# A two-layer hybrid decoder step: index products in units 3 and 4, digits in units 6 to 11, value rows placed on halves of x's parts

## The reference, cut to what matters

```
q, k, v, qi, ki, wi = split(x @ w_in)          # 14 tiles of 128 columns, and 328 more
s = einsum('bqhe,bse->bqhs', qi, ki)           # 8 index heads of width 64
score = einsum('bqhs,bqh->bqs', relu(s), wi) * IDX_SCALE
score = where(key <= query, score, NEG)
_, idx = top_k(score, topk)                    # prompt: 128 of up to 512, sample: 256 of 1025
logits = q . k[idx] * ATTN_SCALE + t5_bias(table, q_pos - idx)
out = softmax(logits) . v[idx]                 # GQA: 16 heads, 4 key heads
x = LN(ALPHA * x + out @ w_out); x = LN(ALPHA * x + relu(x @ w1)^2 @ w2)
```

## Time and profile before

| | |
|---|---|
| median of 3 runs | 1260.26 us |
| the profiled execution's own time | 1260.9 us |
| its span | 1259.1 us |
| PE busy | 1205.1 us (96%), 9582 matmuls |
| DVE busy | 709.0 us (56%) |
| ACT busy | 475.1 us (38%) |
| POOL busy | 82.2 us (7%) |
| mean granted TensorE clock | 0.985 |

### The profile page before, as it was taken

The page is one execution under the profiler, slowest core; times in us unless marked ns, Lnnn a source line. Parts: engine busy times, 40 slices in busy tenths (PEclk is TensorE's granted clock), DMA queues, the critical chain, the costliest instruction groups (busy, mean ns, idle before and its releaser), DMA issues.

```text
span 1259.1 us, 25585 instructions
## 1 busy us (share of the span) xinstructions
PE 1205.1 (96%) x9582; PEld 1109.9 (88%) x9582; DVE 709.0 (56%) x1456; ACT 475.1 (38%) x872; POOL 82.2 (7%) x118
## 2 busy tenths in 40 slices
PE   8998979999999999999999999799999999999995
PEld 4958845589899999999999987598999999999994
DVE  2288889857843443342457767678633433433477
ACT  2342137744532331331334476634422322322332
POOL 4334300100021000000000000000000000000000
PEclk9999989999999999999999999899999999999998
DMA  6687482043222222222233211131222222222221
GB/s 203 192 272 257 124 265 52 21 140 111 68 82 85 96 88 88 96 85 99 84 97 109 82 54 51 52 118 51 68 94 90 87 98 85 99 83 100 84 85 68
DMA packets 61958, 131.00 MB, mean 104 GB/s; under 512 B 7819, under 2 KB 34603, under 8 KB 61755
## 3 DMA queue, kind: packets, MB, share of 16 engines
q1 hardware_dynamic: 47899, 115.16, 28.0%
q10 hardware_dynamic: 10624, 8.26, 2.2%
q0 software_dynamic: 3360, 6.56, 1.7%
HBM read 125.41 MB, written 9.79 MB: 107 GB/s over the span
## 4 chain that ended last, share of the span: by engine, by line
PE 72%; DVE 12%; issue 6%; POOLq 3%; ACT 2%; POOL 2%; SPq 1%; DMA 1%; DVEq 0%; ACTq 0%
PE PS L604 56%; PE PS L634 7%; PE PS L1019 2%; PE PS L792 2%; PE PS L779 2%; PE PS L806 2%; DVE YA L1641 2%; SPq L394 1%; DVE YA L1628 1%; POOLq L385 1%; DVE RSTD L1633 1%; POOL IK L407 1%; POOLq L405 1%; DMA KVX<-cacheV 1%; DVE X L1647 1%
## 5 line engine op out<-in xcount | busy, mean ns | idle before, releaser
L1484 DVE TENSOR_TENSOR WLO<-WRAW,WHI 128x1024 fp32r<-128x1024 f32 x118 | 145.3, 1232 | 322.1 <-ACT WHI L1083 322.0
L1083 ACT ACTIVATE WHI<-WRAW 128x1024 fp32r<-128x1024 f32 x126 | 133.4, 1059 | 390.7 <-PE PS L604 356.9
L604 PE MATMUL PS<-XH,WHI 128*128 128x260 f32 x1184 | 242.3, 286 | 0.9 <-DVE XL L1809 0.7
L604 PE MATMUL PS<-XH,WLO 128*128 128x260 f32 x1184 | 239.9, 285 | 0.0
L604 PE MATMUL PS<-XL,WHI 128*128 128x260 f32 x1184 | 239.8, 284 | 0.0
L604 PE MATMUL PS<-HH,WHI 128*128 128x260 f32 x944 | 191.5, 284 | 0.2 <-DVE HL L1508 0.2
L604 PE MATMUL PS<-HH,WLO 128*128 128x260 f32 x944 | 190.4, 283 | 0.0
L604 PE MATMUL PS<-HL,WHI 128*128 128x260 f32 x944 | 190.2, 283 | 0.0
L604 PEld LDWEIGHTS PS<-XH,WHI 128*128 128x128 f32 x1184 | 183.5, 190 | 6.4 <-issue 5.4
L604 PEld LDWEIGHTS PS<-XH,WLO 128*128 128x128 f32 x1184 | 184.1, 190 | 0.0
L604 PEld LDWEIGHTS PS<-XL,WHI 128*128 128x128 f32 x1184 | 183.6, 190 | 0.0
(11 more groups left out here) (293 smaller groups left out, 1860.5 us busy)
## 6 DMA issues: line engine op xcount, KB each, us to landing
WRAW<-wall SPq DMA_DIRECT2D x168, 512.0 KB, 3.3
bias_skewed<-bias_seq SPq DMA_DIRECT2D x4, 1280.0 KB, 18.7
X<-xT SPq DMA_DIRECT2D x4, 520.0 KB, 6.6
X<-xT SPq DMA_DIRECT2D x1, 2080.0 KB, 11.4
yT<-X SPq DMA_DIRECT2D x8, 260.0 KB
KVB<-cacheK SPq DMA_DIRECT2D x16, 128.0 KB, 3.1
KVX<-cacheK SPq DMA_DIRECT2D x16, 128.0 KB, 2.9
KVB<-cacheK POOLq DMA_DIRECT2D x16, 128.0 KB, 7.3
```

Source lines behind the costliest of these rows:

```text
L604: mm = pe.matmul(PS[:, 2 * slot + g, 0:TG], w[:, slot, k, :], x[:, k, TG * g:TG * g + TG], start=(k == 0 and w is WHI and x is hi), stop=( ...
L1083: nc.scalar.activation(WHI[:, slot], WRAW[:, slot], ACT.Copy).then_inc(hi_done, 1)
L1484: V.tensor_tensor(WLO[:, slot], WRAW[:, slot], WHI[:, slot].bitcast(F32), ALU.subtract).then_inc(lo_dve, 1)
```

## The change

- The index items go head first (the three tiles of head 0, then of head 1, ...): 12 in unit 3 and 12 in unit 4, three at a time at every other piece of a unit, instead of 24 in unit 5. The transposed keys are evicted one unit earlier on ACT.
- The samples' scores and their sum over heads stand within unit 5, ahead of its pieces 2 and 4, instead of ahead of and within unit 6.
- The digits take slots 1 to 11 without a gap (units 6 to 11) instead of 2 to 9 and 12 to 14 (units 7 to 13). ACT reads its page numbers behind the samples' scores instead of ahead of them.
- DVE's low parts of units 4 to 7 stand elsewhere among its work, and the top-k rounds are dealt out anew: 9 rounds before the digits (before: 10), half a round at each digit and step (a whole one, two at the first step), 22 between MSK and QB (5), 5 behind QB (7), 3 (8) and half a round in each attention step from step 5 on (from step 2 on).
- Two of the value samples (8 and 10, `V_HALF`) lie wholly in the first half of XH and of XL; their pages are loaded once the first half of unit 13 has been multiplied. The bias of the diagonal blocks of t = 1 is copied by ACT from BT0 instead of being loaded with the rest, and the load of the rest comes behind the eviction of the samples' probabilities, of which the small one (PNEW) now comes first and has a semaphore of its own.

```diff
-V_LATE = (8, 9, 10, 11, 13, 14, 15)
+V_HALF, V_LATE = (8, 10), (9, 11, 13, 14, 15)
-SLOT_OF = (2, 3, 4, 5, 6, 7, 8, 9, 12, 13, 14)
+SLOT_OF = (1, 2, 3, 4, 5, 6, 7, 8, 9, 10, 11)
...
+        def load_first_values(eng, q, numbers):
+
+            eng.wait_ge(x_used, 1)
+            for n in V_HALF:
+                load_sample(eng, q, n, numbers)
...
+                    if u == A_OUT - 1 and k == KT // 2 - 1:
+                        mm.then_inc(x_used, 1)
...
-            items = [(t, h) for t in range(1, QT) for h in range(IDXH)]
+            items = [(t, h) for h in range(IDXH) for t in range(1, QT)]
...
-                if u == 5:
-                    between = {k: (lambda k=k: index_scores(3 * k, 3 * k + 3))
-                               for k in range(KT)}
-                elif u == 6:
-                    between = {2: sample_sums}
+                if u in (3, 4):
+                    n = 12 * (u - 3)
+                    between = {k: (lambda n=n + 3 * k // 2: index_scores(n, n + 3))
+                               for k in range(0, KT, 2)}
+                elif u == 5:
+                    between = {2: sample_scores, 4: sample_sums}
...
-            act.wait_ge(toe_skew, 16 * 4)
-            act.wait_ge(kv_used, DB)
-            load_bias(1)
             act.wait_ge(dt_mm, 1)
+            nc.scalar.activation(PNEW[:], PS[0:DB, 6, 0:P], ACT.Copy).then_inc(dt_ev, 1)
             nc.scalar.activation(PTD[:].rearrange("p k r -> p (k r)"), PSF[:, 2048:2048 + 1024],
-                                 ACT.Copy)
-            nc.scalar.activation(PNEW[:], PS[0:DB, 6, 0:P], ACT.Copy).then_inc(dt_ev, 1)
+                                 ACT.Copy).then_inc(dt_ev, 1)
+            act.wait_ge(toe_skew, 16 * 4)
+            load_bias(1)
...
-            for u in range(2, 6):
+            for u in range(2, 4):
                 low_part(u, u % 2)
...
-                if n == 8:
-                    low_part(6, 0)
-                if n == 16:
-                    sample_queries()
+                if n == 4:
+                    low_part(4, 0)
+                if n == 13:
+                    low_part(5, 1)
...
-            prompt_rounds(10)
-            low_part(7, 1)
+            low_part(6, 0)
+            prompt_rounds(9)
             dve.wait_ge(ds_ev, 1)
             for r in range(DIGITS):
...
-                prompt_rounds(1)
+                prompt_halves(1)
+                if r == 0:
+                    low_part(7, 1)
                 dve.wait_ge(r_dig, r + 1)
...
-                prompt_rounds(1 if i else 2)
+                prompt_halves(1)
...
-            prompt_rounds(5)
+            prompt_rounds(22)
             dve.wait_ge(z_qb, 2)
...
-            prompt_rounds(7)
+            prompt_rounds(5)
...
                 if i == -1:
-                    prompt_rounds(8)
-                elif i >= 2:
+                    prompt_rounds(3)
+                elif i >= 5:
                     prompt_halves(1)
```

More of the change, by code:

```diff
@@ L213, in program @@
         XL = place("XL", [P, KT, TOK], F32R)
-        KVR = place("KVR", [P, 4, NPG, 256], at=xw)
+        KVR = [place(f"KVR{n}", [P, NPG, 256], at=xw + n * KT // 2 * TOK) for n in range(4)]
         BT = place("BT", [P, NH, 512], at=xw + 16640)
@@ L506, in _ @@
             load_sample(sp, 0, 12, numbers)
+            load_first_values(sp, 0, numbers)
             load_values(sp, 0, numbers)
```

50 lines of the change are left out of this document (32 added, 18 removed).

## The result

| | before | after |
|---|---|---|
| median | 1261.55 us (4 runs, 1258.29 to 1264.9) | 1276.15 us (4 runs, 1272.9 to 1276.68) |
| profiled execution: own time, span | 1260.9, 1259.1 us | 1275.96, 1274.0 us |
| granted clock, mean | 0.985 | 0.982 |

The changed kernel is slower: ratio 1.0109, 95% interval 1.0089 to 1.0128. I had forecast 1264.2 us with a range to 1270, with 0.48 on slower, so the sign of the likeliest case was right, the size 12 us short.

The account below looks back on a forecast made before the run. PE, busy 96% of the span, was taken as the bound. Terms 15.2 + 1.8 - 2.25 - 3.1 - 2.1 - 3.7 - 2.6 = +3.3 us on the profiled 1260.9 gave 1264.2 us, range 1257 to 1270.

Parts of the forecast that it names:

- The change moves them and adds none: Units 3 and 4: the 24 index items cost PE 13.7 us, as they did in unit 5, with no wait added.
- unit 9's delay: Unit 9's load issued at 109.3, weights landing 4.2 us later, start at 117.3: 1.6 us lost.
- the late landings: Rival case: units 9 and 10 take 8.5 us to land, each gap costs 1.7 us of half clock; 1269 us, chance 0.17.
- the pace of the slots: Units 8 to 11: PE's slots set the digits, 3.1 us per half unit with its digit; eleventh at 137, MSK ready at 138.2.
- The 1.88 of before: PE's wait for the indicator at 127.54 goes, against about 1.8 us of new waiting between eighth digit and first step.
- The wait for QB: Ahead of the key products: 22 rounds put QB at 167.5, PE idles 13.7 us, key products start 15.2 us later.
- The half clock at the key products: The beginning of the key products runs at half clock behind the idling: +1.8 us (0 to 3.6).
- PD, first value products and values: Behind the key products: PD's wait goes (-2.25 us), first value products fall to 3.65 (-2.1), the wait on values goes (-3.7).
- POOL's low part of unit 8: Stays at 105.43 for 2.35 us, so unit 8 starts at 107.8 as before, with longer idling in front.
- either about 1.7 us or nothing: Cost in lost clock of one PE idle gap, read from the gaps ahead of unit 8 and of the values.
- the sentence that the trace does not agree at 181.73: Against the skill's advice on idle gaps: products behind 3.73 us of idling, the second 64 value products, ran at full speed.
- the third ("slower still", 1269): Rival: units 9 and 10 land in 8.5 us, each gap costs 1.7 us of half clock, slots 5 us later; chance 0.17.

Follow-up runs that it names:

- the kernel without these two: The changed kernel with index products by head pairs and the skewed bias copies issued ahead of unit 8's load: 1266.1 us median.

## Why the prediction was wrong

Three steps failed. The first is one sentence: of the index items, "The change moves them and adds none". It adds 4.9 us (8 x 2.20 = 17.6 us for the 24 items; before, the eight groups took 12.7). I had carried over the sum of before, in which every item's neighbour lies on the other half of the rows, and did not ask what an item costs without that. It moved the end of the low part of unit 6 from 80.8 to 85.3 and cost 3.3 us in the end.

The second is the cause of unit 9's delay. Its size was half right: load at 109.3 (112.75 in fact) and a landing 4.2 us later, "if the skewed copies are through by then". They were not, and the landing took 5.6 us; issuing the load 13 us sooner did not move it at all. I saw the landing as a duration and not as a place in a queue, and gave the late landings 0.17. A clue was in the rows: 28.5 us between two issues of SP hide how long the 5 MB take. MSK came 9.4 us behind 138.2, and the kernel without these two has it at 138.3, in part by luck, as said above: it lacks the delay of unit 9 that the forecast did hold.

Third, the pace of the slots. Behind unit 8's wait I had counted the half clock (4.8 us for a half unit), behind unit 9's and behind the ninth slot's not ("seventh at 120.4", "Slots 9, 10 and 11 are at 130.9, 134 and 137": 3.1 us each). There it took 4.75 and 4.72: 3.3 us that the sum put at nothing. The trace of before had it: behind the 1.88 us at 127.54 the granted clock is 0.50 from 129.6 to 131.6. And at the ninth slot I had 1.8 us of waiting and it took 3.8; 2.0 of them are the pass that stands beside POOL's low part of unit 11. The 1.88 of before that I let go there was the same thing at another digit.

Slot by slot, the 9.4 us are: 4.7 at the start of unit 9 (122.0 for 117.3), 1.65 of half clock behind it, 1.0 less at unit 10, whose wait came out shorter than forecast, 2.2 at the ninth slot, 1.6 of half clock behind it, and 0.2 after that. In the kernel with the items by pairs, where the first step is mended, 6.1 remain, and only 1.1 of them stand at the start of unit 9.

What was right:
- The wait for QB, 13.7 computed and 13.8 measured, and its cause: with 12 rounds it is gone.
- The half clock at the key products: +1.8 computed. From 176.86 to the first logits at 185.68 they take 8.8 us, against 7.2 before: +1.6.
- PD, first value products and values: 2.25, 2.1 and 3.7 come back (no wait, 3.65 us, no wait). From 176.86 to the third logits at 200.05 PE needs 23.2 us, 9.8 less than the 32.97 of before; I had 9.35 less.
- POOL's low part of unit 8: 106.15 against 105.43. But nobody waits for it, since unit 7 itself ended later; unit 8 begins at 110.41 and not at 107.8.

In numbers, profile against profile (15.1 us, forecast 3.3): of the 11.8 that the forecast lacks, 9.4 stand ahead of QB, the attention gave back 1.9 instead of 2.6 (0.7), from QB to the third logits it was 0.4 better than forecast, and 2.1 lie outside what the change touches: from the attention's last mask product to the end of the span the program took 1005.8 us after the change and 1003.7 before. The granted clock from 766 to 870 us is 0.93 in the one and 0.95 in the other. The kernel before alone shows both, 1003.7 in its first profile and 1005.8 in its second. Over all eighteen profiles this stretch is 1002.2 to 1004.1 us in eight and 1005.6 to 1005.9 in ten; what decides it I did not try, and it stays open. Against the second profile of the kernel before, the changed one is 10.7 us longer instead of 15.1. So "either about 1.7 us or nothing" for a gap was the right kind of term for the half clock, but at 181.73 it differs from run to run, and is no property of the place as I had read it from one profile, and the sentence that the trace does not agree at 181.73 held for that profile only.

Of the rivals the third ("slower still", 1269) came nearest in its mechanism: unit 9 late behind its landing, and half clock behind two of the gaps. Its landing of 8.5 us was not reached for unit 9 (5.6), and it lacked the items and the meeting with POOL. I gave it 0.17.

## What to carry to other kernels

Before moving small matmuls, look whether neighbours lie on different halves of the array's rows: the order inside the group is part of the price. In this kernel a load's landing time belonged to the bytes in front of it; when a step is moved, follow each large transfer that stands behind it, and ask when that one is through, not when the next is issued. Where half clock is charged behind one wait of a chain, charge it behind the others too, unless a row shows full clock there. And profile the kernel before more than once before reading a term of 2 or 3 us from it: two profiles of one kernel differed by 4.4 us.

## What the runs showed of the hardware

- Three products of 64 rows, of widths 256, 384 and 512, take 2.20 us on one half of the rows; 24 items take 12.7 to 12.8 us in alternation and 17.6 in a row.
- A DMA of 512 KB issued behind four copies of 1280 KB landed 18.6 us after its issue, with the same landing moment as one issued 13 us later (5.6 us).
- Behind the same gap of 3.5 to 3.7 us TensorE's clock stayed full in one profile and was at half in another of the same kernel: 3.6 or 6.4 us for 64 products. Behind waits of 5.14 and 3.81 us in the changed kernel it fell to half (0.50 to 0.66), and half a unit took 4.7 us instead of 3.1.
- A VectorE instruction on one element per lane with two operands in SBUF took 0.16 us alone and up to 2.3 us when it began beside GpSimd's subtraction of 2.4 us, and ended with it (129.48 and 129.46). In the kernel before, taking one such meeting away brought the key products 4.3 us forward, and a start 0.1 us behind GpSimd's or 0.3 us ahead of it decides whether they meet.
